# Sample attention's value rounds in pairs: two transposes, then two products

## What is computed

```python
z = (jnp.einsum('bqhd,bkhd->bhqk', q_blk, k) * (SB_HEAD_DIM ** -0.5) + bias[None, :, None, None])
mask = k_pos[None, :] < q_pos[:, None]
log_not = jnp.where(mask, jax.nn.log_sigmoid(-z), 0.0)
between = lax.cumsum(log_not, axis=3, reverse=True) - log_not
a = jnp.where(mask, jnp.exp(jax.nn.log_sigmoid(z) + between), 0.0)
return jnp.einsum('bhqk,bkhd->bqhd', a, v)
```

## Time and profile before

| | us |
|---|---|
| median of 3 runs | 2331.13 |
| lowest, highest | 2331.07, 2333.86 |
| the profiled execution | 2329.63 |
| its span, first to last instruction | 2327.9 |
| PE busy | 2248.4 (97%) |
| DVE busy | 1623.8 (70%) |
| ACT busy | 1060.1 (46%) |
| value products, line 2955, PE busy | 36.2 (34 rounds) |
| weight transposes, line 2943, PE busy | 11.0 (34) |
| first transpose, last product (start) | 1347.73, 1468.99 |

### The profile page before, as it was taken

How to read it: one execution, slowest core, us unless ns; L and a number is a source line. 1 busy time by engine, 2 the same in 40 slices (tenths; PEclk the granted TensorE clock), 3 DMA queues, 4 the chain that set the end, 5 groups by cost and what they waited for, 6 DMA issues and landing times. The chain is left out here.

```text
span 2327.9 us, 43422 instructions
## 1 busy us (share of the span) xinstructions
PE 2248.4 (97%) x16494; PEld 1849.0 (79%) x16494; DVE 1623.8 (70%) x2755; ACT 1060.1 (46%) x1975; POOL 47.3 (2%) x107
## 2 busy tenths in 40 slices
PE   8999999999999999999989888999999999999998
PEld 8888888877879888888877665678977777777786
DVE  7676666757885487677667997556766766655886
ACT  7332232334564667566646564435422232324453
POOL 0000000000000100000010010010000000000000
PEclk9999999999999999999999999999999999999999
DMA  5343342465464445344448989532243432437354
GB/s 163 104 154 104 111 138 93 136 208 190 134 206 136 97 112 115 91 97 114 88 136 295 312 275 347 163 101 90 61 161 94 153 104 94 144 122 261 110 172 147
DMA packets 390830, 345.37 MB, mean 148 GB/s; under 512 B 105593, under 2 KB 298489, under 8 KB 390672
## 3 DMA queue, kind: packets, MB, share of 16 engines
q1 hardware_dynamic: 390672, 343.21, 47.7%
HBM read 271.54 MB, written 88.38 MB: 155 GB/s over the span
## 5 line engine op out<-in xcount | busy, mean ns | idle before, releaser
L1344 PE MATMUL a_q<-a_uh,a_p_hi 128*128 128x352 f32 x672 | 233.4, 347 | 0.6 <-ACT a_xp L1435 0.6
L1346 PE MATMUL a_q<-a_uh,a_p_lo 128*128 128x352 f32 x672 | 216.3, 322 | 0.0
L1345 PE MATMUL a_q<-a_ul,a_p_hi 128*128 128x352 f32 x672 | 215.9, 321 | 0.0
L1344 PEld LDWEIGHTS a_q<-a_uh,a_p_hi 128*128 128x128 f32 x672 | 126.5, 188 | 23.6 <-issue 21.7
L1345 PEld LDWEIGHTS a_q<-a_ul,a_p_hi 128*128 128x128 f32 x672 | 127.0, 189 | 0.1
L1346 PEld LDWEIGHTS a_q<-a_uh,a_p_lo 128*128 128x128 f32 x672 | 126.1, 188 | 0.0
L980 PE MATMUL c_q<-c_b_hi,c_a_hi 128*128 128x512 f32 x264 | 105.3, 399 | 3.6 <-DVE c_a_lo L879 2.3
L980 PE MATMUL a_q<-a_b_hi,a_a_hi 128*128 128x512 f32 x264 | 103.5, 392 | 2.0 <-DVE a_a_lo L879 1.8
L981 PE MATMUL c_q<-c_b_hi,c_a_lo 128*128 128x512 f32 x264 | 104.7, 397 | 0.0
L982 PE MATMUL c_q<-c_b_lo,c_a_hi 128*128 128x512 f32 x264 | 104.4, 395 | 0.0
L982 PE MATMUL a_q<-a_b_lo,a_a_hi 128*128 128x512 f32 x264 | 102.8, 389 | 0.0
(11 more groups left out here) (773 smaller groups left out, 6499.0 us busy)
## 6 DMA issues: line engine op xcount, KB each, us to landing
w_page<-in_cache_v SPq DMA_DIRECT2D x128, 256.0 KB, 4.4
a_w_raw<-in_ffn_gu SPq DMA_DIRECT2D x44, 512.0 KB, 5.1
c_w_raw<-in_ffn_gu SPq DMA_DIRECT2D x44, 512.0 KB, 5.0
a_a_raw<-hid_rows SPq DMA_DIRECT2D x66, 256.0 KB, 2.7
c_a_raw<-hid_rows SPq DMA_DIRECT2D x66, 256.0 KB, 2.7
k_blocks<-in_cache_k SPq DMA_DIRECT2D x64, 256.0 KB, 3.6
w_page<-in_cache_k SPq DMA_DIRECT2D x64, 256.0 KB, 4.0
w_page<-k_blocks SPq DMA_DIRECT2D x64, 256.0 KB, 5.0
```

The source lines that it names most:

```text
L1344: nc.tensor.matmul(self.pm[at % 2][:, 0:TB], wh, self.uh[t][:, c], start=(c == 0), stop=False)
L1345: nc.tensor.matmul(self.pm[at % 2][:, 0:TB], wh, self.ul[t][:, c], start=False, stop=False)
L1346: mm = nc.tensor.matmul(self.pm[at % 2][:, 0:TB], wl, self.uh[t][:, c], start=False, stop=(c == KC - 1))
```

## The change

TensorE's value rounds are ordered in pairs (0 and 1, 2 and 3, up to 32 and 33). At the time at which the first round of the pair was transposed, both are transposed, one behind the other. At the time of the second round's product, both products are made, one behind the other. What each transpose and product waits for is as it was; the rest of TensorE's program and the other engines' programs are untouched. The lines of what follows in the file move by 13, and the products are line 2959 afterwards.

```diff
             def values():
-                for r, (gi, p) in enumerate(ALL_ROUNDS):
-                    keys = P if p < PAGES else T_S
-                    yield value_time(gi, p) + PE_AT["values"][0]
...
-                    nc.tensor.transpose(flat(pw[r % 2])[0:keys, 0:P], ex[:, gi, p * P:p * P + keys], ident[:]).then_inc(E("w_turned"), 1)
-                    yield value_time(gi, p) + PE_AT["values"][1]
-                    pe.wait_ge(E("wt_copied"), r + 1)
...
-                    mm.then_inc(E("v_mm"), 1)
+                for r in range(0, G * ROUNDS, 2):
+                    yield value_time(*ALL_ROUNDS[r]) + PE_AT["values"][0]
+                    turn_weights(r)
+                    turn_weights(r + 1)
+                    yield value_time(*ALL_ROUNDS[r + 1]) + PE_AT["values"][1]
+                    weigh_values(r)
+                    weigh_values(r + 1)
                 yield value_time(G, 0) + PE_AT["values"][2]
```

`turn_weights` and `weigh_values` hold the old loop's two pieces, with the same waits:

```diff
+            def weigh_values(r):
+
+                gi, p = ALL_ROUNDS[r]
+                keys = P if p < PAGES else T_S
+                pe.wait_ge(E("wt_copied"), r + 1)
+                if p == 0:
+                    pe.wait_ge(E("k_copied0"), 2 * len(KEY_ROUNDS))
+                    at_least(pe, E("o_kept"), gi)
+                n = len(KEY_ROUNDS) + PAGES * gi + p
+                if p < PAGES:
+                    wait_page(pe, n)
...
+                mm.then_inc(E("v_mm"), 1)
```

More of the change, by code:

```diff
@@ L2933, in scores @@
                         products(flat(pz[r % 2])[:, 0:T_S], gi, lambda b, c: (ks, ks_b)[b % 2][:, c])
-            def values():
-                for r, (gi, p) in enumerate(ALL_ROUNDS):
-                    keys = P if p < PAGES else T_S
-                    yield value_time(gi, p) + PE_AT["values"][0]
[L2939 to L2942, removed]
-                    nc.tensor.transpose(flat(pw[r % 2])[0:keys, 0:P], ex[:, gi, p * P:p * P + keys], ident[:]).then_inc(E("w_turned"), 1)
-                    yield value_time(gi, p) + PE_AT["values"][1]
-                    pe.wait_ge(E("wt_copied"), r + 1)
[L2946 to L2956, removed]
-                    mm.then_inc(E("v_mm"), 1)
@@ new lines, in turn_weights @@
+            def turn_weights(r):
+                gi, p = ALL_ROUNDS[r]
+                keys = P if p < PAGES else T_S
+                if p == 0:
+                    pe.wait_ge(E("weighted"), gi + 1)
+                    pe.wait_ge(E("z_out"), G * ROUNDS)
+                at_least(pe, E("wt_copied"), r - 1)
+                nc.tensor.transpose(flat(pw[r % 2])[0:keys, 0:P], ex[:, gi, p * P:p * P + keys], ident[:]).then_inc(E("w_turned"), 1)
+            def weigh_values(r):
+                gi, p = ALL_ROUNDS[r]
+                keys = P if p < PAGES else T_S
+                pe.wait_ge(E("wt_copied"), r + 1)
+                if p == 0:
+                    pe.wait_ge(E("k_copied0"), 2 * len(KEY_ROUNDS))
[3 more added lines that the diff above has]
+                    wait_page(pe, n)
+                elif gi == 0:
+                    pe.wait_ge(E("v_new_in"), 16)
+                for b in range(4):
+                    mm = nc.tensor.matmul(pv[R * b:R * b + R, :], wt[0:keys, r % 2, R * b:R * b + R],
+                                          page[n % SLOTS][:, b] if p < PAGES else v_new[:], start=(p == 0), stop=(p == PAGES))
+                mm.then_inc(E("v_mm"), 1)
```

## The result

| | before | changed |
|---|---|---|
| median of the runs | 2331.38 us (6 runs, 2327.05 to 2333.86) | 2340.76 us (6 runs, 2337.61 to 2344.45) |
| ratio | | 1.0047, 95% interval 1.0033 to 1.0061 |
| profiled execution, span | 2327.9 us | 2337.3 us |
| the value rounds, from round 0's transpose to the block L89 behind the gather | 124.61 us | 137.48 us |

The kernel became slower, by 9.4 us between the medians and 7.7 to 14.2 us by the interval. I had forecast +5.8. In the rest of the text "the stretch" is the last row of the table. It grew by 12.87 us, the span by 9.4: the changed execution reached the stretch 0.38 earlier and took 3.09 less behind it (852.50 us against 855.59). There the granted clock fell three times for 3.4 us in the execution of before (1485.5, 1622.0, 2164.7) and once in the changed one (1632.4), besides the span's last microseconds.

A forecast was written before the change was run, and what follows sets the result against it. TensorE was taken as nearly the bound in the value rounds, its queue holding the delta rule's chain in order. +1.4 + 3.0 + 1.4 = +5.8 us gave 2336.9 us, range 2331.0 to 2341.0.

The forecast's parts named there:

- first group: Rounds 0 to 15: chain links left bare cost 4.4 us, less idle times removed and pair savings; net +1.4 us.
- pair across the groups: Rounds 16 and 17 share one bank; VectorE's keep and the run behind it come late; net +3.0 us, bounds 0.9 to 4.0.
- second group and the end: Later rounds to the last pair: bare links cost 3.7 us, less filled waits and 1.7 saved; net +1.4 us.
- price list: TensorE timeline prices for products, transposes and bare links, such as 1.00 us a product, read at a granted clock of 1.00.
- Rival 2: At rounds 16 and 17 the keep costs only its own wait, 0.9 us; sum 3.7, 2334.8 us; chance 0.22.
- Savings: In each of 17 pairs, one tile-shape change fewer and a cheaper second transpose: 0.19 us a pair, 3.2 in all.
- Pages: Page loads for the value products: lead unchanged, SyncE has time, so counted at nothing.
- Rival 1: Value rounds: the block of two is simply denser, only the 3.2 us of switches is left; 2327.9 us, chance 0.08.
- Rival 3: Value rounds: pages come late, three pairs wait 1.5 us each; 2341.4 us, chance 0.10.

The follow-up runs named there:

- e_first_fill: e_first with transposes of the identity into an unused bank ahead of five waits; stretch 127.15 us, ratio 1.0012 to the kernel before.
- e_cross: Changed kernel with only rounds 16 and 17 paired, the other 32 one by one as before; stretch 128.50 us, ratio 1.0024 to the kernel before.
- e_second: Changed kernel with pairs in rounds 18 to 33 only, rounds 0 to 17 one by one; stretch 128.21 us, ratio 1.0011 to the kernel before.
- e_split: Changed kernel with rounds 16 and 17 taken apart, the other 16 pairs kept; stretch 132.71 us, ratio 1.0033 to the kernel before.
- e_first: Changed kernel with pairs in rounds 0 to 15 only, later rounds one by one; stretch 131.49 us, ratio 1.0018 to the kernel before.
- e_bank: Changed kernel with the second group accumulating in another bank, so round 17 waits for no keep; stretch 135.96 us, ratio 1.0045 to the kernel before.
- e_prods: Changed kernel with only the products paired, each transpose back at its own time; stretch 132.29 us, executed once, no ratio.
- e_fill: Changed kernel with identity transposes ahead of L2853, L2859, round 17 and in the last chunk; stretch 136.53 us, ratio 1.0029 to the kernel before.
- e_fill_all: Changed kernel with identity transposes ahead of 30 waits; stretch 139.71 us, ratio 1.0046 to the kernel before.
- e_fill_most: Changed kernel with identity transposes ahead of the larger waits only; stretch 135.77 us, ratio 1.0052 to the kernel before.
- e_fill_split: e_fill_all with rounds 16 and 17 taken apart; stretch 134.46 us, ratio 1.0044 to the kernel before.

## Why the prediction was wrong

The direction was right and so were most causes, but the sum left out a term of about its own size.

| step | forecast | runs |
|---|---|---|
| first group | +1.4 | +1.7 (e_first_fill) |
| pair across the groups | +3.0 | +2.4 (e_cross) |
| second group and the end | +1.4 | +2.3 (e_second, e_split) |
| sum at a clock of 1.00 | +5.8 | +6.4 |
| the clock | none | 12.87 - 6.4 = 6.5 in the first execution, 11.34 - 6.4 = 4.9 in the second; 5.8 estimated from the timed runs |

- **The step that failed** is the price list, "at a granted clock of 1.00". I read 1.00 in the windows of before and took it into the new order, while forecasting that TensorE would idle 9 us more there. The idle came in long waits close together (0.63 and 1.64 us ahead of L2853 and L2859 of the fifth chunk), the clock fell to 1.2 GHz behind them, and the matmuls of the chain took up to 1.8 times as long (L2803, 2.07 for 1.16 us). No rival had it either, so the range ended at 2341.0. The ratio puts the changed kernel at 2331.13 x 1.0047 = 2342.1; the bare median, 2340.76, stands just inside. The last row of the table is a difference of pieces from several executions, with their unexplained idle times in it (2.4 us in the stretch before, 0.6 in the changed kernel's first execution); e_first_fill against e_first shows the price in one comparison, about 4 us in the first group.
- *First group*: right in size, in part by luck. The list missed the wait of 1.23 ahead of an L2821, and it counted 0.5 where round 16 stood, which e_first_fill leaves as it was. In the changed kernel the fifth chunk's L2891 was 3.5 late, and what is above 1.1 came with the fall at 1390.0.
- *Pair across the groups*: right in cause, 0.6 too high in size. VectorE's row behind the keep sets it, 5.6 us forecast from round 16 to L2853, 5.67 to 5.79 measured in three executions (6.26 in the changed kernel's first, where L2803 was slow as well). Rival 2 fell with e_bank.
- *Second group*: too low by 0.9. I had no term for L2821's wait for VectorE's inverse, 0.60 each in two chunks of that group.
- *Savings*: product to product takes 0.88 (0.9 forecast); as a sum I can't separate them. With the transposes alone paired no gain can be measured.
- *Pages*: in the changed kernel no product waited, but in its first execution round 15's page landed only 0.29 us ahead of its product. In e_split that product waited 1.74, in e_prods 0.39, in e_fill, e_fill_all, e_fill_most and e_fill_split 0.6 to 1.5. The lead that I called unchanged was too thin there to be counted at nothing.
- *Rival 1* (denser, not slower) is out: the covers were worth more than the switches. *Rival 3* gave nearly the right time (2341.4) for the wrong reason: no page was late.

The Trainium skill, TensorE: Matmul & The Clock Gate, section HAM oscillation — how this bites in real kernels, prices time at the low clock at half of its length. By that, as an estimate, the first execution would have lost 12.0 us to its 23.9 us at half and the second 6.9 to 13.7. The runs here show 6.5 and 4.9; in e_cross the fall at the pair cost next to nothing, because the slow work ran where TensorE would have waited anyway.

## What to carry to other kernels

Work that stands between dependent steps of a chain is cover, and grouping it for fewer switches lays the chain's waits bare; in a queue that hands work to and fro, count the links that lose their cover before the switches that are saved. When an edit adds idle time to TensorE in long pieces close together, price it twice: once as waiting, and once as a clock that may fall behind it, in the windows of the stretch and not in the mean of the span. Keep the last use of an accumulator away from its next first use: the engine that empties it has a queue of its own, and everything behind the emptying becomes late too.

## What the runs showed of the hardware that I had not expected

- Single idle times of 1.2 to 1.8 us on a TensorE that is otherwise busy were followed by a fall to half clock in 7 of 11 executions at one place, and by none of 5 once transposes of the identity filled them.
- The same program fell at different places in two executions (1390.0, 1417.3 and 1471.9 in one, 1381.8, 1392.0 and 1422.8 in the other), so that one profile at 1.00 does not say that the next one will be.
- A fall's price depends on its place: next to nothing for 3.4 us at half at the pair in e_cross, where VectorE was the bound, 0.9 for the 3.4 us at 1393.5 in the same execution, some 4 us for 10.2 us at half in e_first, where the chain ran through TensorE.
- TensorE's idle times that no wait explains stand earlier in the program where instructions are added ahead of them: 1.32 us at the sixth chunk's L2847 before, 1.78 at L2836 in e_first_fill and e_fill_most, 2.08 and 1.98 at L2830 in e_fill_all and e_fill_split. In these four executions the clock fell within 1.8 us behind them; what they are is not shown.
